# Order of the first loads, the step sizes' layout, and the place of the first norm in a two-block kernel

## What is computed

```python
mod = jax.nn.silu(c) @ ada_w[l] + ada_b[l]
sh1, sc1, g1, sh2, sc2, g2 = jnp.split(mod, 6, axis=-1)
hn = rmsnorm(h, mix_pre_g[l]) * (1.0 + sc1[:, None, :]) + sh1[:, None, :]
proj = hn @ w_in[l]
q, k, v, og, a_lr, u = jnp.split(proj, SPLITS, axis=-1)
log_a = jax.nn.log_sigmoid(a_lr @ w_alpha[l] + b_alpha[l]) / GLA_TAU
o = gla_chunked(q, k, v, log_a)          # gated linear attention
dt = jnp.exp(s5_log_dt)[:, None]         # 32 groups, one step size each
mag = jnp.exp(lam_re * dt)               # S5: a diagonal state space model, 64 states a group
```

## Time and profile before

| | us |
|---|---|
| median of 3 executions | 3577.45 (3575.67 to 3578.99) |
| the profiled execution | 3579.49 |
| its span, first to last instruction | 3577.7 |

### The profile page before, as it was taken

One profiled execution on the slowest core, in us unless ns is written; L12 is line 12 of the kernel. 1 busy time (PEld: TensorE's weight loads), 2 busy tenths in 40 slices (PEclk: granted clock), 3 DMA queues, 4 the chain that ended last, 5 costly groups with the idle time before them and its releaser, 6 DMA issues.

```text
span 3577.7 us, 33491 instructions
## 1 busy us (share of the span) xinstructions
PE 3186.9 (89%) x13492; PEld 1528.5 (43%) x13493; DVE 1169.6 (33%) x2030; ACT 520.2 (15%) x990; POOL 268.4 (8%) x352
## 2 busy tenths in 40 slices
PE   5967678999999999999994988787878999999998
PEld 2442234444443333333332644456556444444444
DVE  1348952332233332323233247324143001212201
ACT  1211012100000000010102124213133000100000
POOL 0026521000000000000000003000000000000000
PEclk8969778799999999999996899987889999999999
DMA  9216331699999999999982110110100222121210
GB/s 273 71 33 235 139 108 36 222 326 338 335 328 353 357 353 356 351 361 348 356 326 84 48 36 1 42 36 1 48 1 1 71 83 94 65 76 59 77 65 24
DMA packets 287682, 582.43 MB, mean 163 GB/s; under 512 B 7953, under 2 KB 12492, under 8 KB 287500
## 3 DMA queue, kind: packets, MB, share of 16 engines
q1 hardware_dynamic: 281328, 562.19, 44.0%
q0 software_dynamic: 5072, 15.80, 1.9%
q10 hardware_dynamic: 1132, 2.30, 0.2%
HBM read 576.08 MB, written 4.19 MB: 162 GB/s over the span
## 4 chain that ended last, share of the span: by engine, by line
PE 79%; DVE 13%; ACT 3%; issue 2%; DMA 1%; POOL 1%; SPq 0%; DVEq 0%; ACTq 0%; PEldq 0%; POOLq 0%
PE psum_all L211 76%; DVE scratch L1235 4%; PE psum_all L219 3%; DVE hidden L2078 2%; DMA panel<-in_ada_w 1%; DVE scratch L1259 1%; DVE scratch L3140 1%; DVE scratch L1252 1%; ACT scratch L3202 1%; DVE scratch L2726 1%; SPq L188 0%; ACT hidden L433 0%; DVE resid L1331 0%; ACT scratch L410 0%; ACT scratch L412 0%
## 5 line engine op out<-in xcount | busy, mean ns | idle before, releaser
L211 PE MATMUL psum_all<-panel,scratch 128*64 128x512 f32 (+3 forms) x5568 | 977.0, 507 | 1.4 <-ACTq L1853 0.8
L211 PE MATMUL psum_all<-hidden,panel 128*128 128x512 f32 (+1 forms) x1808 | 796.9, 602 | 21.5 <-ACT hidden L433 10.9
L211 PEld LDWEIGHTS psum_all<-hidden,panel 128*128 128x128 f32 (+1 forms) x1808 | 347.3, 193 | 462.3 <-issue 444.2
L211 PEld LDWEIGHTS psum_all<-panel,scratch 128*64 128x64 f32 (+2 forms) x5568 | 333.7, 131 | 472.2 <-issue 425.6
L211 PE MATMUL psum_all<-scratch 128*128 128x64 f32 (+8 forms) x1512 | 366.7, 440 | 111.6 <-DVEq L1273 63.6
L211 PEld LDWEIGHTS psum_all<-scratch 128*128 128x128 f32 (+2 forms) x1512 | 232.0, 234 | 212.9 <-DVEq L1273 77.0
L2078 DVE TENSOR_TENSOR hidden<-hidden,psum_all 128x512 f32<-128x512 f32 x264 | 169.7, 684 | 290.5 <-PE psum_all L211 290.5
L211 PE MATMUL psum_all<-scratch,panel 128*128 128x512 f32 (+1 forms) x672 | 250.5, 531 | 2.0 <-DVE resid L3327 1.0
L219 PE MATMUL psum_all<-const,scratch 128*128 128x128 f32 (+4 forms) x954 | 151.7, 298 | 84.1 <-ACTq L3214 22.8
L219 PEld LDWEIGHTS psum_all<-const,scratch 128*128 128x128 f32 (+4 forms) x954 | 110.5, 156 | 185.1 <-issue 84.0
L211 PEld LDWEIGHTS psum_all<-scratch,panel 128*128 128x128 f32 x672 | 127.5, 190 | 127.5 <-issue 119.6
(11 more groups left out here) (314 smaller groups left out, 2219.1 us busy)
## 6 DMA issues: line engine op xcount, KB each, us to landing
panel<-in_exp_w_gu SPq DMA_DIRECT2D x132, 2048.0 KB, 11.9
panel<-in_exp_w_down SPq DMA_DIRECT2D x66, 2048.0 KB, 14.2
panel<-in_w_in SPq DMA_DIRECT2D x17, 2048.0 KB, 8.5
panel<-in_ada_w SPq DMA_DIRECT2D x12, 2048.0 KB, 9.1
panel<-in_w_mod SPq DMA_DIRECT2D x12, 2048.0 KB, 8.0
panel<-in_ffn_w_gate SPq DMA_DIRECT2D x5, 2048.0 KB, 7.8
panel<-in_ffn_w_up SPq DMA_DIRECT2D x5, 2048.0 KB, 7.8
panel<-in_w_out SPq DMA_DIRECT2D x4, 2048.0 KB, 7.9
```

The costliest lines, as they stand in the source:

```text
L211: ins = self.pe.matmul(out, lhsT, rhs, start=start, stop=stop)
```

## The change

Four things are done.

- The tokens are loaded by SP, behind the constants and ahead of the panels.
- `s5_log_dt` is loaded as one column of 32 values on 32 partitions, at once. DVE makes from the identity matrix which group has which parity and which pair, multiplies by the column, and PE spreads the values to 2 x 64 partitions with two small matmuls into a bank of `to_act`, between the low-rank gate and the value projection. ACT's Exp reads that bank.
- The squares of the first norm follow each tile's copy, PE sums them between modulation rows 0 and 1, and ACT takes the root there. The shift stays behind the modulation.
- GpSimd waits for `alr_ready` (the low-rank projection is copied) ahead of the eight row loads of the second block.

```diff
@@ act_norm, now in three parts @@
+            act_norm_root(act, step, std, n, dim)
+            act_norm_shifts(act, kt, shifts, dst)
@@ pe_first_mods @@
                 if p:
                     pe_mod_turn(pe, mm, to_act, mod_rows[(p - 1) % 2], 1)
+                else:
+                    pe_norm(pe, mm, n_sq, T, DT)
@@ ACT @@
+        def act_first_squares(act):
+            for k in range(DT):
+                act.wait_ge(resid_tile.sem, resid_tile.next(act))
+                act.activation(n_sq[:, k, :], resid[:, k, :], ACT.Square).then_inc(sq_ready.sem, 1)
+            act.wait_ge(resid_ready.sem, resid_ready.next(act))
...
+                else:
+                    act_norm_root(act, step, n_std, T, D)
@@ sp_first_loads @@
             sp.dma_start(const[:, :], a["const"]).then_inc(const_loaded.sem, 16)
+            sp.dma_start(x_tok, a["x"][0].rearrange("(t p) d -> p t d", p=P)).then_inc(x_loaded.sem, 16)
@@ act_first_loads @@
-            act.dma_start(x_tok, a["x"][0].rearrange("(t p) d -> p t d", p=P)).then_inc(x_loaded.sem, 16)
@@ dve_turn_inputs @@
-            dve.wait_ge(to_dve.free, to_dve.own_reads())
+                dve.wait_ge(to_dve.free, to_dve.own_reads())
+                dve.sem_inc(resid_tile.sem, 1)
+            dve.wait_ge(resid_tile.sem, resid_tile.next(dve, DT))
             dve.sem_inc(resid_ready.sem, 1)
             dve_turn_rows(dve, step, [1, 2])
+            dve_s5_steps(dve, step)
@@ pe_gla, ahead of the value projection @@
+            pe_s5_steps(pe, mm)
@@ step sizes @@
         def pool_s5_steps(pool):
-            pool.wait_ge(x_loaded.sem, x_loaded.next(pool, 16))
-            for half in range(2):
-                pool.dma_start(s5c[64 * half:64 * half + 64, S5_DT, :],
-                               a["s5_log_dt"].rearrange("a (g two) -> two a g", two=2)[half]
-                               .broadcast_to([64, S5_PAIRS]),
-                               allow_slow_non_contiguous=True).then_inc(s5_steps.sem, 16)
+            pool.dma_start(log_dt, a["s5_log_dt"].rearrange("a (g n) -> (a g) n", n=1),
+                           allow_slow_non_contiguous=True).then_inc(s5_steps.sem, 16)
+
+        def dve_s5_steps(dve, step):
+            groups = ident[0:2 * S5_PAIRS, 0:2 * S5_PAIRS]
+            dve.tensor_reduce(of_parity, groups.rearrange("p (g two) -> p two g", two=2), AX_X, ALU.add).then_inc(dve_done, 1)
+            dve.tensor_reduce(of_pair, groups.rearrange("p (g two) -> p g two", two=2), AX_X, ALU.add).then_inc(dve_done, 1)
+            dve.wait_ge(dve_done, step.next(2))
+            dve.wait_ge(s5_steps.sem, s5_steps.next(dve, 16))
+            dve.tensor_scalar(dt_of_pair, of_pair, log_dt, None, ALU.mult).then_inc(dve_done, 1)
+            dve.wait_ge(dve_done, step.next())
+            dve.sem_inc(s5_spread.sem, 1)
+
+        def pe_s5_steps(pe, mm):
+            pe.wait_ge(s5_spread.sem, s5_spread.next(pe))
+            pe.wait_ge(to_act.free, to_act.room())
+            bank = to_act.fill()
+            for two in range(2):
+                ins = mm(bank[64 * two:64 * two + 64, 0:S5_PAIRS], of_parity[:, two:two + 1].broadcast_to([2 * S5_PAIRS, 64]),
+                         dt_of_pair)
+            ins.then_inc(to_act.full, 1)
@@ act_s5_angles @@
-            act.wait_ge(s5_steps.sem, s5_steps.next(act, 32))
-            act.activation(v(S5_DT), v(S5_DT), ACT.Exp).then_inc(act_done, 1)
-            act.wait_ge(act_done, step.next())
+            act.wait_ge(to_act.full, to_act.next_full())
+            bank = to_act.take()
+            act.activation(v(S5_DT), bank[:, 0:S5_PAIRS], ACT.Exp).then_inc(to_act.free, 1)
+            act.wait_ge(to_act.free, to_act.own_reads())
@@ programs of the engines @@
             pool_s5_steps(pool)
+            pool.wait_ge(alr_ready.sem, alr_ready.next(pool))
             pool_row_loads(pool)
...
             pe_first_mods(pe, mm)
-            pe_norm(pe, mm, n_sq, T, DT)
...
-            act_first_mods(act)
             act.preload_act_table_set(LN_EXP)
-            act.wait_ge(resid_ready.sem, resid_ready.next(act))
-            act_norm(act, step, resid[:, :, :], n_sq, n_std, T, DT, D,
-                     [mods[:, k, :] for k in range(DT)], hidden)
+            act_first_squares(act)
+            act_first_mods(act, step)
+            act_norm_shifts(act, DT, [mods[:, k, :] for k in range(DT)], hidden)
```

More of the change, by code:

```diff
@@ L391, in build @@
         s5_steps = signal("s5_steps")
+        s5_spread = signal("s5_spread")
         s5_blocks = signal("s5_blocks")
@@ L425, in act_norm, with act_norm_shifts, act_norm_root @@
                 act.activation(sq[:, k, :], src[:, k, :], ACT.Square).then_inc(sq_ready.sem, 1)
+            act_norm_root(act, step, std, n, dim)
+            act_norm_shifts(act, kt, shifts, dst)
+        def act_norm_shifts(act, kt, shifts, dst):
+            if shifts is not None:
+                for k in range(kt):
+                    act.wait_ge(scaled.sem, scaled.next(act))
+                    act.activation(dst[:, k, :], dst[:, k, :], ACT.Identity, bias=shifts[k]).then_inc(normed.sem, 1)
+        def act_norm_root(act, step, std, n, dim):
             act.wait_ge(to_act.full, to_act.next_full())
@@ L429, in act_norm @@
             act.sem_inc(std_ready.sem, 1)
[L430 to L433, removed]
         def pe_norm(pe, mm, sq, n, kt):
@@ L534, in pe_first_mods, with act_first_mods @@
                     pe_mod_turn(pe, mm, to_act, mod_rows[(p - 1) % 2], 1)
+                else:
+                    pe_norm(pe, mm, n_sq, T, DT)
             pe_mod_turn(pe, mm, to_act, mod_rows[(FIRST_PANELS - 1) % 2], 1)
-        def act_first_mods(act):
+        def act_first_squares(act):
[3 more added lines that the diff above has]
+            act.wait_ge(resid_ready.sem, resid_ready.next(act))
+        def act_first_mods(act, step):
             for p in range(FIRST_PANELS):
@@ L942, in build @@
         mod_banks = Banks(psum[2:4], sem("mod_banks_full"), sem("mod_banks_free"))
+        log_dt = small[0:2 * S5_PAIRS, 56:57]
+        of_parity, of_pair = small[0:2 * S5_PAIRS, 57:59], small[0:2 * S5_PAIRS, 60:76]
+        dt_of_pair = small[0:2 * S5_PAIRS, 76:92]
         def pool_s5_steps(pool):
-            pool.wait_ge(x_loaded.sem, x_loaded.next(pool, 16))
-            for half in range(2):
-                pool.dma_start(s5c[64 * half:64 * half + 64, S5_DT, :],
-                               a["s5_log_dt"].rearrange("a (g two) -> two a g", two=2)[half]
-                               .broadcast_to([64, S5_PAIRS]),
-                               allow_slow_non_contiguous=True).then_inc(s5_steps.sem, 16)
+            pool.dma_start(log_dt, a["s5_log_dt"].rearrange("a (g n) -> (a g) n", n=1),
[17 more added lines that the diff above has]
+            ins.then_inc(to_act.full, 1)
         def pool_s5_loads(pool):
```

## The result

The changed kernel takes **3541.86 us** (median of four executions, 3534.11 to 3549.7) against 3576.56 for the kernel before beside it: 0.9902 of its time, interval 0.9879 to 0.9925. The profiled execution took 3534.11 (span 3532.3, mean clock 0.930), that of the kernel before 3579.49 (span 3577.7, clock 0.920). So the two traces lie 45 us apart, 11 more than the medians: some of what they show belongs to these two executions and not to the two kernels.

A forecast was written before the change was run, and what follows sets the result against it. Head bound by modulation panels delayed by a transfer hole, then the first norm. Scaling from 69.97 to 40.0 gives 30.0, less 0.1 for DVE and 0.6 on PE: 29.3 us, 3548.2; range 3543 to 3559.

The forecast's parts named there:

- Whose hole it is: Transfers at 22 to 40 us, 37 GB/s: two log_dt loads hold each engine twice, 7.1 and about 7.6 us.
- B: Rival: the hole belongs to the moment, not log_dt, and stays; only the norm's 12.4 us won, 3565; chance 0.08.
- C: Rival: the log_dt column still holds the engines 7.1 us at the start; 3555; chance 0.05.
- D: Rival: DVE waits for the log_dt column ahead of the factors; slower, 3593; chance 0.01.
- Panel 3: Last first modulation panel lands at 34.4 us instead of 52.13; bounds 32.7 to 35.4.
- Norm ahead of the rows: Before modulation row 1: norm's sum takes 6.9 us to 27.3, PE ready 1.1 us before panel 3, no path cost.
- the tokens' move: Tokens behind the constants on SP's queue: no cost to panel 3, tokens land at 12.5 us.
- After panel 3: Row 3 to factors: 4.8 us plus 0.8, half the slow clock case's 1.6; scaling from 40.0 instead of 69.97.
- The spread: Two small matmuls, four passes, ahead of the value projection: 0.6 us on PE's path, range 0.5 to 2.0.
- GpSimd's wait: Wait for alr_ready ahead of eight small loads that only the second block reads: nobody waits.
- the shift goes through: Stages after the head: the head's 29.3 us gain reaches the end unchanged, 2 us either way.
- The scatter: Measurement noise, taken from three times of 3575.67 to 3578.99; 0.2% (7 us) told from no change.

The follow-up runs named there:

- dt_only: Kernel before with only the log_dt column, its spread and GpSimd's later row loads: 3554.0 us, 0.9942.
- after_old_dt: Changed kernel with the two strided log_dt loads again and no spread, GpSimd's wait for alr_ready kept: 3564.0 us, 0.9966.
- old_half: Changed kernel with only the first of the two strided log_dt loads, a constant for the odd groups, no spread: 3551.3 us.
- the trace of after: First profiled execution of the changed kernel, 3534.11 us; median of its four executions 3541.86 us.
- the three traces: Profiles of the unedited changed kernel: the first and two repeats; medians 3541.86, 3537.0 and 3544.3 us.
- before_b: Kernel before once more, unedited: 3575.25 us (eleven executions).
- before_d4: Kernel before with four idle DVE copies between A1 and the scaling, where DVE waits anyway: 3574.6 us, 1.0001.
- The idle copies: Kernel before with one, three or four unread DVE copies between the chunk stage's first two copies: 3573.2, 3573.0 and 3572.3 us.
- after_again: Changed kernel once more, unedited: 3537.0 us (four executions).
- before_g3: Kernel before with three idle DVE copies between the chunk stage's first two copies: 3573.0 us, 0.9992.
- before_g4: Kernel before with four idle DVE copies between the chunk stage's first two copies: 3572.3 us, 0.9996.
- parity: Changed kernel with three empty fills that return the to_act bank rotation to its old place: 3556.1 us.

## Why the prediction was right in the head and wrong in the sum

- **Whose hole it is: right.** `dt_only` takes the hole away, `after_old_dt` brings it back, `old_half` brings back half. Rivals B and C (hole stays, column holds the engines) fall: GpSimd's queue takes 0.9% of 0 to 60 in the trace of after, and the column landed 6.4 us after its issue. D falls with that, DVE never waited for it. The reading of 32 packets with 64 elements each was right. The estimate of 14.7 us for each engine from the earlier trace rows is a little low, since its second window caught eight packets alone: over 16 to 38 us the same queue has 72.0% of 16 engines, 15.8 us for each, and 16.2 when repeated in `after_old_dt`.
- **Panel 3: right.** Forecast 34.4; row 3 started at 34.35, 35.26 and 34.17 in the three traces.
- **Norm ahead of the rows: right.** Row 0 at 18.97 (forecast 18.5), the sum of 7.13 us (6.9) to 27.95 (27.3), PE ready 0.31, 2.41 and 0.84 us ahead of the panel in the three traces (1.1). The margin was thin: with the tokens on the old queue it is gone. Counting the tokens' move as free was right as a cost; that the norm depends on it, and what it is worth, 2 to 3.5 us, was not said.
- **After panel 3: right on average.** Scaling forecast at 40.0, measured 39.05, 41.6 and 40.6. The middle between the two clock cases, 0.8 us, was the right choice: both came.
- **The spread: half of it.** 0.29 us for four passes (forecast 0.6), 0.07 us each, below both rows that the forecast took it from (0.13 and 0.49 us a pass).
- **GpSimd's wait: nobody waited for it**, as forecast.
- **The step that failed: "the shift goes through", with "2 us either way for clocks and rates of the later stages".** At 193.1 the three traces have 29.7, 24.9 and 26.0 us, 26.9 on average, against 29.3 forecast. Between the scaling and that point they lost 1.2, 3.5 and 3.4 us, of which 0.2 is the spread: the first projections took 37.07, 37.53 and 37.50 us instead of 36.03, and the value projection 27.73, 29.43 and 29.43 instead of 27.73. The mean clock over the first projections was 0.94, 0.92 and 0.92, and 0.96 before. From there to the end the traces gain 15.7, 6.6 and 7.3 more, where `before_b` and `before_d4` gain 3.4 and 3.0 too: the execution that the shifts are counted against is one of the longest. In the executions the whole difference is 33.8 us with a standard error of 1.8. With 26.9 of it ahead of 193.1, the later stages, put at 0 with 2 either way, give about 7 us on average, and single executions lie 6 to either side. The loss ahead of that point and the gain behind it partly cancel, so the number came closer than its two parts.
- **The scatter.** It was taken from three times within 3.3 us. The kernel before spreads over 15 us and the changed one over 20. A margin of 2 us was too small for stages with a mean clock of 0.61 and 0.69 in the trace of before, whichever way the mechanism went.

What is shown: the chunk stage's time depends on how its work lies against the stretches of low clock. The idle copies made it 0.3 to 1.6 us shorter without any work being taken away, 1.7 to 3.5 us less their own delays. In the three traces of the changed kernel the stage gives 3.3, 1.8 and 1.8 us, 2.3 of the 7. What isn't shown: where the other 4 to 5 us on average come from. In the trace of after 7.4 us arise in the first attention, but there `after_again` loses 0.6 us, and `before_b`, without any edit, gains 3.1. The idle copies gave their traces 6.2 to 9.7 us from 193.1 to the end, 3 of which the repeats of before gain as well, and their mean times only 1 to 2.4. So this rest may be the clock's again, in the late stages, or something else that the new head leaves behind, other than the banks. No run tells the two apart.

## What to carry to other kernels

Look for DMAs of single elements by the time that their packets take, not by their bytes: 8 KB in 4-byte pieces held up 387 GB/s for some 16 us, and here 32 contiguous numbers with a small spread on PE replaced them for 0.3 us. A norm that needs only the input belongs in the wait for the weights, but check that the input itself comes ahead of them. And where a stage's mean granted clock lies between 0.5 and 1.0, don't count on a shift passing through it unchanged: give it several us either way, take the scatter from ten executions or more, and place the profiled execution within it before you take a sum against it.

## What was not expected of the hardware

- Two loads of 1024 single 4-byte elements each on GpSimd's queue held each of the 16 DMA engines for 16.2 us (`after_old_dt`) and stopped the panels behind them. The time lay in packets of 64 elements, 7.8 us each on average in `old_half`; packets of two elements on the same queue took 0.009 us (after). From ACT's queue the same loads went as about 2200 packets of 4 bytes, stopped nothing and held the rate at 158 to 175 GB/s from 20 to 38 us.
- Useless work made a stage shorter: 1.9 us of idle copies took the chunk stage from 50.5 to 48.9 us, by the place of the low clock.
- Executions of one kernel differ with the mean granted clock: 3534.1 us at 0.930, 3549.7 at 0.925. The changed kernel has twice the scatter of the kernel before (standard deviation 6.5 against 2.9 us). That is no mark of the new head: `before_g3` and `before_g4` have 4.6 and 5.4, `dt_only` 3.0, `old_half` 1.4 (four executions).
- In `parity` six small matmuls and three readings more in the head went with a gap 6.6 us longer behind the experts, 1.8 ms later, with four more DMAs of instructions. It is one trace.
